# Moving the reciprocal softmax sums of two attention stages: by transfers through device memory in one, in pairs through GpSimd in the other

## The reference, cut to what matters

```python
s = jnp.einsum('bqkgd,bnkd->bkgqn', q_blk, k, preferred_element_type=jnp.float32) * scale
p = jax.nn.softmax(s, axis=-1).astype(v.dtype)
return jnp.einsum('bkgqn,bnkd->bqkgd', p, v)
...
y_l = (o_l.reshape(h_lat.shape[:2] + (GQA_WIDTH,)) * jax.nn.silu(g_l)) @ w_out
```

## Time and profile before

| what | value |
|---|---|
| median of 3 runs | 1556.99 us (1556.64 to 1563.7) |
| the profiled execution's own time | 1555.47 us |
| its span | 1553.7 us |
| mean granted TensorE clock | 0.987 |
| PE, DVE, ACT, POOL busy | 97%, 64%, 52%, 28% of the span |

### The profile page before, as it was taken

One profiled execution on the slowest core, in us unless ns is written; L12 is line 12 of the kernel. 1 busy time (PEld: TensorE's weight loads), 2 busy tenths in 40 slices (PEclk: granted clock), 3 DMA queues, 4 the chain that ended last, 5 costly groups with the idle time before them and its releaser, 6 DMA issues. The chain is left out here.

```text
span 1553.7 us, 26405 instructions
## 1 busy us (share of the span) xinstructions
PE 1504.4 (97%) x9547; PEld 1320.2 (85%) x9547; DVE 1001.2 (64%) x2144; ACT 813.9 (52%) x1869; POOL 434.1 (28%) x507
## 2 busy tenths in 40 slices
PE   6999999999999999989999999999997999999998
PEld 3787878897998899978888888889997889999996
DVE  4665636428888888863448966575222887777783
ACT  5322321127777777755554433343112987777773
POOL 1022201002222111100121333220480554555552
PEclk9899999999999999999999999999998999999999
DMA  9444425409111254023233444579857998999872
GB/s 361 141 136 141 144 82 177 159 18 272 25 25 24 86 157 136 17 91 102 81 123 120 134 140 144 151 211 289 263 137 238 289 290 256 264 254 267 255 227 68
DMA packets 195654, 252.24 MB, mean 162 GB/s; under 512 B 32979, under 2 KB 157477, under 8 KB 195493
## 3 DMA queue, kind: packets, MB, share of 16 engines
q1 hardware_dynamic: 193076, 242.16, 51.4%
q10 hardware_dynamic: 2448, 8.39, 1.8%
HBM read 187.59 MB, written 78.76 MB: 171 GB/s over the span
## 5 line engine op out<-in xcount | busy, mean ns | idle before, releaser
L2537 DVE CUSTOM_DVE_ANT_0 nprob<-nS,bias_set 128x640 f32<-128x640 f32 x128 | 105.2, 822 | 68.3 <-PE nS L2375 45.6
L1152 ACT ACTIVATE prob<-S,nm,qk_inv 128x512 f32<-128x512 f32 (+1 forms) x208 | 146.4, 707 | 3.5 <-DVE nm L1088 3.5
L576 PE MATMUL pp<-h_hi,w_hi 128*128 128x512 f32 (+1 forms) x408 | 147.5, 361 | 0.0
L577 PE MATMUL pp<-h_lo,w_hi 128*128 128x512 f32 (+1 forms) x408 | 144.5, 354 | 0.0
L578 PE MATMUL pp<-h_hi,w_lo 128*128 128x512 f32 (+1 forms) x408 | 144.4, 354 | 0.0
L1106 DVE TENSOR_TENSOR ptlo<-TB,pthi 128x512 fp32r<-128x512 f32 (+1 forms) x192 | 114.8, 598 | 29.7 <-ACT pthi L1164 27.9
L2456 ACT CAST npt_hi<-nTB 128x256 fp32r<-128x256 f32 (+1 forms) x256 | 103.3, 426 | 56.8 <-PE nTB L2386 53.1
L1164 ACT CAST pthi<-TB 128x512 fp32r<-128x512 f32 (+1 forms) x192 | 99.2, 517 | 63.1 <-PE TB L1033 62.9
L1081 DVE TENSOR_REDUCE mx<-S 128x1 f32<-128x512 f32 (+1 forms) x208 | 116.7, 580 | 10.6 <-PE S L1025 9.4
L2550 DVE TENSOR_TENSOR npt_lo<-nTB,npt_hi 128x256 fp32r<-128x256 f32 (+1 forms) x256 | 114.9, 483 | 2.6 <-ACT npt_hi L2456 1.4
L2447 ACT ACTIVATE nprob<-nprob,selector 128x640 f32<-128x640 f32 x128 | 106.6, 833 | 11.4 <-DVE selector L2537 10.4
(11 more groups left out here) (324 smaller groups left out, 4519.9 us busy)
## 6 DMA issues: line engine op xcount, KB each, us to landing
kq_scratch<-p_stage SPq DMA_DIRECT2D x96, 256.0 KB, 3.9
keys<-kq_scratch SPq DMA_DIRECT2D x32, 768.0 KB, 4.8
bias_set<-bias_scratch SPq DMA_DIRECT2D x64, 384.0 KB, 6.3
v_strip<-v_scratch SPq DMA_DIRECT2D x128, 128.0 KB, 5.3
wearly<-in_mod_w SPq DMA_DIRECT2D x15, 1024.0 KB, 8.2
bias_scratch<-bias_wide_scratch SPq DMA_DIRECT2D x16, 768.0 KB, 11.0
w_raw<-in_na_w_in SPq DMA_DIRECT2D x11, 1024.0 KB, 5.5
wside<-in_mod_w SPq DMA_DIRECT2D x9, 1024.0 KB, 7.1
```

Source lines behind the costliest of these rows:

```text
L576: pe.matmul(acc, whi[:, k, ws], hi[:, k, a:a + width], start=(k == 0), stop=False)
L577: pe.matmul(acc, whi[:, k, ws], lo[:, k, a:a + width], start=False, stop=False)
L1152: act.activation(prob[:, p % 5, a:a + n], S[:, score_bank(p, k), 0:n], ACT.Exp, bias=nm[:, p % 5:p % 5 + 1], scale=q_scale(h - 1, p) if p ...
```

## The change

**Grouped attention.** PE's two transposes per group and DVE's copy go. Instead SP's queue has, for each n, a store of the group's 128 x 2 reciprocals to a row in device memory (after `recd`), a wait for its landing, and a load of the 256 values broadcast to 128 partitions into one of two buffers; DVE's `out` waits for the load. The gate loads and the bias table's small and large transfers, which stood in batches behind gate loads, are dealt out: three small ones in each of n = 0 to 15, one large one in each of n = 17 to 32. The fills stay where they were, ahead of the store of n = 0.

**Last stage.** POOL writes each group's two reciprocal columns 64 times over (`replicate`) into a tile that holds both heads of the unit; PE turns that tile once per unit, two transposes in place of four, before the second group's product. ACT's inverse copy and POOL's two multiplications run once per unit on 128 partitions. The gate has two buffers and semaphores of its own, and is loaded last in a unit. A wait for `replicate` is added before DVE's reciprocal.

```diff
@@ grouped attention, SP @@
                 bias_fill(sp, io, filled, tabled)
-                for h in range(1, QH):
-                    load(h)
-                    if h == 1:
+
+                def store_inverses(n):
+
+                    q = 2 * (n % GQA_GROUPS)
+                    sp.wait_ge(recd, n + 1)
+                    if n >= GQA_GROUPS:
+                        inverses_moved(sp, inv_in, n - GQA_GROUPS)
+                    sp.dma_start(inverse_row(n).rearrange("(p s) -> p s", s=2), rec[:, q:q + 2]).then_inc(inv_out[n % 2], 16)
+
+                def load_inverses(n):
+
+                    inverses_moved(sp, inv_out, n)
+                    if n >= 2:
+                        sp.wait_ge(od, n - 1)
+                    sp.dma_start(inv[:, n % 2, :], inverse_row(n).rearrange("(a n) -> a n", a=1).broadcast_to([P, 256])
+                                 ).then_inc(inv_in[n % 2], 16)
+
+                for n in range(QH * GQA_GROUPS):
+                    store_inverses(n)
+                    load_inverses(n)
+                    if n % GQA_GROUPS == 0 and n:
+                        load(n // GQA_GROUPS)
+                    if n == 0:
                         sp.wait_ge(filled, 16)
-                    if h <= KINDS:
-                        bias_space(sp, io, h - 1, spaced)
-                    if h == KINDS + 1:
+                    for i in range(3 * n, min(3 * n + 3, KINDS * STRIP_W)):
+                        bias_space(sp, io, i // STRIP_W, i % STRIP_W, spaced)
+                    if n == ROWS_FROM:
                         sp.wait_ge(spaced, 16 * KINDS * STRIP_W)
-                    if KINDS < h <= KINDS + HALVES:
-                        bias_rows(sp, io, h - KINDS - 1, tabled)
+                    if ROWS_FROM <= n < ROWS_FROM + HALVES * 8:
+                        bias_rows(sp, io, *divmod(n - ROWS_FROM, 8), tabled)
@@ grouped attention, product (PE) @@
-                        at_least(pe, recd, GQA_GROUPS, h, gr)
                         at_least(pe, od, GQA_GROUPS, h, gr - 1)
-                        for s in range(2):
-                            pe.transpose(O[:, 256 + s * P:256 + (s + 1) * P],
-                                         rec[:, q - 1 + s:q + s].broadcast_to([P, P]), consts["ident"][:, :])
@@ grouped attention, out (DVE) @@
-                    dve.tensor_copy(inv[:, :], O[:, 256:512]).then_inc(invd, 1)
-                    at_least(dve, invd, GQA_GROUPS, h, gr)
-                    dve.tensor_tensor(qk[:, bass.ds(head, 1), tok:tok + 256].rearrange("p a n -> p (a n)"),
-                                      O[:, 0:256], inv[:, :], ALU.mult).then_inc(od, 1)
+                    n = GQA_GROUPS * h + gr
+                    inverses_moved(dve, inv_in, n)
+                    dve.tensor_tensor(qk[:, bass.ds(head, 1), tok:tok + 256].rearrange("p a (s n) -> p (a s) n", s=2),
+                                      O[:, 0:256].rearrange("p (s n) -> p s n", s=2),
+                                      inv[:, n % 2, :].rearrange("p (n s) -> p s n", s=2), ALU.mult).then_inc(od, 1)
@@ last stage, PE @@
+                def spread_inverses(u):
+
+                    pe.wait_ge(repd, 2 * u + 2)
+                    if u:
+                        pe.wait_ge(invd, u)
+                    for f in range(HALVES):
+                        pe.transpose(O[:, 1, 256 + f * P:256 + (f + 1) * P],
+                                            both[u % 2][:, f, :, :].rearrange("p a n -> p (a n)"), consts["ident"][:, :])
@@ last stage, fold (ACT) @@
                     if gr >= 2:
-                        act.wait_ge(od, gr - 1)
-                    act.copy(inv[rows(a), :], O[rows(a), gr % 2, 256:512]).then_inc(invd, 1)
+                        act.wait_ge(od, gr // 2)
+                    if a == 1:
+                        act.copy(inv[:, :], O[:, 1, 256:512]).then_inc(invd, 1)
@@ last stage, POOL @@
+                def replicate(gr):
+                    if gr >= 2 * UNITS:
+                        return
+                    u, a = gr // 2, gr % 2
+                    pool.wait_ge(recd, 2 * gr + 2)
+                    if u >= 2:
+                        pool.wait_ge(pvd, 2 * u - 2)
+                    at = 2 * gr % 8
+                    pool.tensor_copy(both[u % 2][:, :, a, :],
+                                     rec[:, at:at + 2].unsqueeze(2).broadcast_to([P, HALVES, 64])).then_inc(repd, 1)
+                    pool.wait_ge(repd, gr + 1)
```

More of the change, by code:

```diff
@@ L858, in bias_fill, with bias_space, bias_rows @@
                 sp.dma_start(bias_place(io)[:, f, r, :, a:b], io["mask_cols"][:, :, 0:b - a]).then_inc(tabled, 16)
-def bias_space(sp, io, kind, spaced):
+def bias_space(sp, io, kind, c, spaced):
     shift = (0, -8, -16)[kind]
[L864 to L870, removed]
-    taps = io["bias_wide"].rearrange("h k c e w -> (h k) c (e w)")
[L873 to L877, removed]
+    k0 = (max(c - 8, 0), c, min(8 + c, 16))[kind]
+    at = k0 + shift - c + GRID_W - 1
+    sp.dma_start(io["bias_wide"][:, kind, c, :, k0:k0 + KW], io["bias"][:, :, at:at + KW]).then_inc(spaced, 16)
+def bias_rows(sp, io, f, r, tabled):
+    taps = io["bias_wide"].rearrange("h k c e w -> (h k) c (e w)")
+    v0 = first_key_row(f, r)
+    e0 = v0 + 4 * f - (8 * f + r) + KH - 1
+    sp.dma_start(bias_place(io)[:, f, r, :, v0 * KEY_W:(v0 + KH) * KEY_W],
+                 taps[:, :, e0 * KEY_W:(e0 + KH) * KEY_W]).then_inc(tabled, 16)
 GQA_TILES = [(NCTX + P * j, T) for j in range(NLAT // P)] + [(P * j, NCTX) for j in range(CT)]
@@ L950, in grouped_attention @@
         topd = c.sem("g_max_raw")
-        totd, recd, gated, invd = c.sem("g_total"), c.sem("g_recip"), c.sem("g_gated"), c.sem("g_inv")
+        totd, recd, gated = c.sem("g_total"), c.sem("g_recip"), c.sem("g_gated")
+        inv_out, inv_in = ([c.sem(f"g_inv_{x}{i}") for i in range(2)] for x in ("stored", "loaded"))
         td, hid, lod = c.sem("g_turned"), c.sem("g_pt_hi"), c.sem("g_pt_lo")
@@ L2249, in neighbourhood_and_out @@
             inv, o = (c.sb(f"n_{x}", [P, 256]) for x in ("inv", "o"))
+        with c.place((205.5, 207)):
+            both = [both0, c.sb("n_rec_both1", [P, HALVES, 2, 64])]
         vs = c.sb("v_strip", [P, 2, 6, 256], F32R)
@@ L2269, in neighbourhood_and_out @@
         meand, rootd, late, switched = c.sem("x2_mean"), c.sem("x2_root_done"), c.sem("x2_late_root"), c.sem("root_table_in")
-        lated = c.sem("x2_late_recip")
+        gin = [c.sem(f"gate_in{i}") for i in range(2)]
+        lated, repd = c.sem("x2_late_recip"), c.sem("n_rec_spread")
         x_last, st_last = [c.sem(f"x1_last_in{b}") for b in range(2)], [c.sem(f"x_last_stored{b}") for b in range(2)]
@@ L2648, in _ @@
                 swap(1)
[L2649 to L2656, removed]
-                    pool.wait_ge(invd, gr + 1)
-                    if a == 0:
-                        pool.wait_ge(vl[slot], 96 * (gr // 4 + 1))
-                    if gr >= 2:
-                        pool.wait_ge(od, gr - 1)
-                    pool.tensor_tensor(inv[rows(a), :], inv[rows(a), :], g[rows(a), gr // 2 % 3, :], ALU.mult).then_inc(gid, 1)
-                    pool.wait_ge(gid, gr + 1)
-                    pool.wait_ge(sumd, gr + 1)
-                    if a == 0 and gr >= 2:
-                        pool.wait_ge(old, gr // 2)
-                    pool.tensor_tensor(o[rows(a), :], half[rows(a), :], inv[rows(a), :], ALU.mult).then_inc(od, 1)
-                    if a == 1:
-                        u = gr // 2
-                        pool.wait_ge(od, gr + 1)
-                        if s >= 2:
-                            pool.wait_ge(om, 32 * (s - 2) + 32)
-                        hi, lo = (o_[:, s % 2, i, :].rearrange("p (h r c) -> p r h c", h=2, c=8) for o_ in (ohi, olo))
-                        raw = o[:, :].rearrange("p (r h c) -> p r h c", h=2, c=8)
-                        pool.tensor_copy(hi, raw).then_inc(ohd, 1)
-                        pool.wait_ge(ohd, u + 1)
-                        pool.tensor_tensor(lo, raw, hi, ALU.subtract).then_inc(old, 1)
@@ new lines, in _ @@
+                replicate(0)
+                replicate(1)
+                for u in range(UNITS):
+                    s, i, slot = u // PAIRS, u % PAIRS, u % 2
+                    if u:
+                        pool.wait_ge(old, u)
+                    swap(u + 2)
+                    if u >= 12 and u % 4 == 0:
+                        root(u // 4 - 3)
+                    replicate(2 * u + 2)
+                    pool.wait_ge(invd, u + 1)
+                    pool.wait_ge(gin[slot], 16 * (u // 2 + 1))
+                    pool.tensor_tensor(inv[:, :], inv[:, :], g[:, u % 2, :], ALU.mult).then_inc(gid, 1)
+                    pool.wait_ge(gid, u + 1)
+                    replicate(2 * u + 3)
+                    pool.wait_ge(sumd, 2 * u + 2)
+                    pool.tensor_tensor(o[:, :], half[:, :], inv[:, :], ALU.mult).then_inc(od, 1)
+                    pool.wait_ge(od, u + 1)
+                    if s >= 2:
```

(6 more changed lines are left out.)

37 lines of the change are left out of this document (23 added, 14 removed).

## The result

| what | before | changed |
|---|---|---|
| median | 1556.99 us | 1574.47 us (1572.81 to 1578.61, 4 runs) |
| ratio of the runs, 95% interval | | 1.0115 (1.0092 to 1.0138) |
| the profiled execution's own time, span | 1555.5, 1553.7 us | 1573.7, 1571.9 us |
| mean granted TensorE clock | 0.987 | 0.978 |

The kernel is slower by 17.5 us. 1556.4 was forecast, with a range up to 1565.5.

A forecast was written before the change was run, and what follows sets the result against it. PE was taken as the bound (busy 97%), except in the last stage's first strip. -13.7 + 16.2 + 2.7 - 5.8 = -0.6 us takes 1555.5 to 1554.9; with 1.5 for the runs' median, 1556.4, range 1549.3 to 1565.5.

The forecast's parts named there:

- After that the groups' transfers are early ... I put it at nothing: Grouped attention after the first stall: store, wait and load stay under 12.3 us, also beside large transfers; cost nothing.
- Rival C: Grouped attention, groups 17 to 32: store plus load behind large transfers repeatedly exceed 12.3 us; +9.6 us, 1566; chance 0.13.
- The prediction's own sign of being wrong: Grouped attention: DVE waiting for loads in groups 17 to 32 would show the forecast wrong; no size given.
- The stall: Start of grouped attention: first store waits behind the fills on SP, so PE stands; +16.2 us, bounds +13.0 to +19.
- Clock: Grouped attention, after the stall: PE runs at 1.2 GHz for about 5.4 us; +2.7 us (1 to 3.6).
- Small transfers: Grouped attention: store and load land in 2.3 us each; store, wait and load together take 5.2 us, hidden.
- Per group: Grouped attention: 0.22 us per group without transposes (8.8), plus shorter PE waits and an earlier last output (4.9); -13.7 us.
- The last stage: Last stage: 0.21 us less per unit by losing a transpose pair, POOL's added copies hidden; -5.8 us in all.
- A: Whole kernel, the forecast case: two small gains against one stall, 1556.4 us, own range 1550.5 to 1564; chance 0.60.

## Why the prediction was wrong

**The step that failed** is "After that the groups' transfers are early ... I put it at nothing". It set store plus load, 11.1 us beside a large transfer, against the 12.3 us from reciprocal to output, and found that it fits. It does: from the store's issue the medians are 7.4 + 3.8 = 11.2. That is a latency. But SP stands still while a store lands, and the next large transfer and the next store wait behind that wait. The same paragraph had the store land 8.5 us after its reciprocal and the group's time at 8.0; that alone says that each group starts later than the one before. Its 5.2 us from reciprocal to the large transfer's issue also hold for the first of the sixteen alone; the next can be issued only behind that late landing. Measured, the cycle is 9.4 us, and it cost 11.4 us between outputs 20 and 33, plus the 2.6 us that 13 groups would have won. Two runs show it: by PE, the middle loses nothing; by another order with the same transfers and nearly the same latency, the lateness stops growing. A third, with the large transfers on another queue, shows that the queue is not what makes the stores slow. Rival C named this loss, with a landing of 12.2 us as the point from which it decides. The large transfers landed in 8.5 us in the median and it came all the same, so the point of decision was wrong, and with it the chance of 0.13. The prediction's own sign of being wrong, DVE waiting for loads in groups 17 to 32, is what the trace shows.

**Sizes.** The stall: expected +16.2, PE's wait is 16.65 us and output 0 is 17.6 late; nearly right, with the store landing at 389.8 (expected 390.0) and the output at 393.5 (393.1 was its expected end). The prediction excluded an early landing by a rule of the Trainium skill (DMA: Bandwidth & Descriptors, Queues, rings and completion order), that a completion lands only behind all earlier writes of its engine. The trace agrees: the last fill landed at 389.6, the store just behind it. *Clock:* expected +2.7 from 5.4 us at half speed; the clock is 0.50 for the first 2.8 us of PE's work, half of which is 1.4. The 17.6 of the list holds it: PE stood 16.65 us, DVE's output 0 is 17.6 late, and output 1, behind the slow microseconds, is 17.5 late. That the clock rose so soon here is luck: behind the same stall it stayed at 0.50 for 5.8 us with the bias transfers between store and load. *Small transfers:* taken at 2.3 us from issue to landing, after transfers of 15 KB; store and load together have these figures (us, minimum, median, maximum), the large ones' neighbours included:

```profile
DMA to landing us min/median/max: 2.6/4.2/9.7
```

In the quiet last group that made 8.5 us of an expected 5.2, and cost 2.5 us where 0.8 were left. The 2.0 us that the prediction's sentence on the Trainium skill (DMA: Bandwidth & Descriptors, Anatomy of one DMA) gives are stated there for transfers that GpSimd issues; these are issued by SP, and none took under 2.6. *Per group:* expected 0.22 and a share of the waits, -13.7 us in all; 0.20 came, which over 40 groups would be -8. The 0.22 is there in every group. Here is the product's start without transposes, against the earlier trace rows: 0.24 from L1053, then 0.12 with no switch.

```profile
506.58 0.40 PE L1053 MATMUL S<-k_hi,qlo 128*128 128x512 f32 x1
506.82 0.28 PE L1079 MATMUL O<-pthi,v_hi 128*128 128x256 f32 x1
506.94 0.28 PE L1080 MATMUL O<-ptlo,v_hi 128*128 128x256 f32 x1
```

The 0.44 us wait of each head is gone as well, but the very next turn then starts 0.28 us later than it could, and a step two groups on gives back another 0.22. Of 1.5 us per head, 1.0 remains. So the removed wait was partly cover for another.

**The last stage** was right in mechanism and size: 0.21 to 0.26 per unit, -5.1 us alone by the ratio, POOL's copies 0.29 us and never waited for by PE.

**The sum again** with what was measured, from the two traces: +17.4 before the first output (the changed kernel's stage starts 0.2 us later, which makes the 17.6), -3.9 to output 20, +11.4 to output 33, -1.8 to output 38, +2.5 in the last, +0.8 between the stages, -8.4 in the last stage (some 3 of it chance), +0.2 at the start: 18.2, the difference of the spans. Two of the prediction's side sums don't close: with its own last stage the lower end of A is -13.7 + 13.0 + 1 - 5.8 = -5.5, not -6.4, and +9.7 on 1557.0 is 1566.7, not 1564. Neither touches the forecast.

## What to carry to other kernels

A store and load through memory has two costs that are checked apart: its latency against the slack of the value, and the time that the issuing queue is blocked against the period of the loop. The second adds up, the first doesn't. Put what else the queue has to issue between the store and the wait for it, not between the load and the next store (here that took 11.7 us off the lateness), and look at what stands in the queue when the loop begins: its first trip pays for all of it.

## What the runs showed of the hardware that was not expected

A store of 128 pieces of 8 bytes (1 KB) takes 2.7 to 4.9 us until its load can be issued when nothing large is in flight, and 5.6 to 9.7 behind a transfer of 768 KB on the same queue (changed kernel, groups 18 to 33). It takes 3.6 to 9.0 when the large transfer is issued behind it on the same queue (both runs with that order), and 4.3 to 9.3 when it is on ACT's queue. The median landings are 7.4 us in the changed kernel and 5.5 to 5.9 in the others. With a gate load of 640 KB ahead as well it took 7.5 to 9.7 in all four kernels. So the one issued earlier is slowed too, and a queue of its own does not shield it. It works the other way as well: the same large transfers, at the same pace, land in 8.5 us with a store and a load beside each and in 5.1 without. What in the memory path does it was not tried.

The clock after one and the same stall of some 17 us stayed at 0.50 for 2.8 us of PE's work in one trace and for 5.8 in another.
